# Hybrid decoder step on one core: embedding products around the routing's rank and table, and two pieces of VectorE work moved

## What is computed

```
x = x + token_mix(rmsnorm(x))               # convolution and retention heads
h = rmsnorm(x)
gate, eid = top-1 of 4 groups, then top-2 of its 8 experts, per token
x = x + sum over the 2 picks of gate * (silu(h Wg[e]) * (h Wu[e])) Wd[e]    # 32 experts
ple = rmsnorm(p @ w_ple)                    # the embedding product
x = x + ple * sigmoid(x @ w_ple_gate);  y = rmsnorm(x)
```

## Time and profile before

| | us |
|---|---|
| median of 3 runs | 692.29 (692.18 to 695.29) |
| profiled execution | 691.82 |
| its span, first to last instruction | 690.0 |
| TensorE, VectorE, ScalarE, GpSimd busy | 661.9, 575.8, 405.4, 259.7 |
| mean granted TensorE clock | 0.987 of full |

### The profile page before, as it was taken

One profiled execution on the slowest core, in us unless ns is written; L12 is line 12 of the kernel. 1 busy time (PEld: TensorE's weight loads), 2 busy tenths in 40 slices (PEclk: granted clock), 3 DMA queues, 4 the chain that ended last, 5 costly groups with the idle time before them and its releaser, 6 DMA issues.

```text
span 690.0 us, 12915 instructions
## 1 busy us (share of the span) xinstructions
PE 661.9 (96%) x4714; PEld 605.8 (88%) x4714; DVE 575.8 (83%) x808; ACT 405.4 (59%) x521; POOL 259.7 (38%) x182
## 2 busy tenths in 40 slices
PE   7999999998999999997999999999999999998995
PEld 5899999998998979956899999999999999876885
DVE  5499999996866484476889999999999999969785
ACT  7331242227263042366789999999999999853322
POOL 1131588979428330005233333333333333320001
PEclk9999999999999999989999999999999999999998
DMA  9641432112019263536699999999999999676211
GB/s 292 200 139 19 150 111 74 62 63 73 1 65 343 85 217 120 207 144 210 258 341 376 371 364 371 361 369 379 384 392 387 381 388 382 251 312 207 77 61 62
DMA packets 49534, 156.14 MB, mean 226 GB/s; under 512 B 6938, under 2 KB 28634, under 8 KB 36427
## 3 DMA queue, kind: packets, MB, share of 16 engines
q1 hardware_dynamic: 35905, 133.98, 52.3%
q10 hardware_dynamic: 9346, 12.13, 5.2%
q0 software_dynamic: 4240, 9.44, 4.0%
HBM read 143.55 MB, written 17.59 MB: 234 GB/s over the span
## 4 chain that ended last, share of the span: by engine, by line
PE 73%; DVE 9%; issue 5%; POOL 4%; DMA 4%; ACT 2%; ACTq 0%; SPq 0%; POOLq 0%; DVEq 0%
PE bank L606 70%; PE bank L610 4%; DMA out<-front 1%; DMA catT<-expert_rows 1%; DVE front L1756 1%; POOL uext L2289 1%; DVE front L1757 1%; DVE z L1392 1%; DVE front L1783 1%; DVE z L1564 1%; POOL z L2376 1%; DVE z L1700 1%; DMA scratch<-h_rows,sorted_tok 1%; POOL grs L2369 1%; POOL uext L2288 1%
## 5 line engine op out<-in xcount | busy, mean ns | idle before, releaser
L1425 DVE TENSOR_TENSOR ring_parts<-ring,catT_parts 128x2048 fp32r<-128x2048 f32 x64 | 146.2, 2285 | 0.6 <-ACT catT_parts L2016 0.5
L2016 ACT ACTIVATE catT_parts<-ring 128x2048 fp32r<-128x2048 f32 x64 | 123.3, 1926 | 5.7 <-PE bank L606 5.7
L606 PE MATMUL bank<-ring_parts,hT_high 128*128 128x256 f32 (+1 forms) x748 | 113.7, 296 | 0.0
L2422 POOL DMA_INDIRECT expert_rows<-scratch,cur_code x32 | 40.8, 1274 | 172.3 <-issue 121.5
L606 PEld LDWEIGHTS bank<-ring_parts,hT_high 128*128 128x128 f32 x748 | 100.6, 189 | 4.0 <-DVE ring_parts L1295 0.2
L1264 DVE SCALAR_TENSOR_TENSOR bank<-uext,cpar,bank 128x512 f32<-128x512 f32 x116 | 87.4, 753 | 0.0
L1614 DVE TENSOR_TENSOR ring_parts<-ring,down_high 128x2048 fp32r<-128x2048 f32 x30 | 68.8, 2293 | 8.1 <-ACT down_high L2118 7.4
L2269 POOL TENSOR_TENSOR ring_parts<-ring,ring_parts 128x2048 fp32r<-128x2048 f32 x11 | 51.7, 4701 | 60.0 <-ACT ring_parts L1831 60.0
L606 PE MATMUL bank<-ring_parts,catT_parts 128*128 128x256 f32 x480 | 69.2, 282 | 2.5 <-DVE front_parts L1321 1.3
L606 PE MATMUL bank<-catT_parts,xT_odd 128*128 128x256 f32 x512 | 67.8, 285 | 0.0
L2398 POOL COPY cur_code<-codes 128x1 int32 (+1 forms) x32 | 63.2, 1976 | 7.9 <-DVE tokidx L1551 7.7
(11 more groups left out here) (342 smaller groups left out, 1318.5 us busy)
## 6 DMA issues: line engine op xcount, KB each, us to landing
ring<-in_w_expert_gate SPq DMA_DIRECT2D x32, 1024.0 KB, 5.5
ring<-in_w_expert_up SPq DMA_DIRECT2D x32, 1024.0 KB, 5.8
ring<-in_w_expert_down SPq DMA_DIRECT2D x32, 1024.0 KB, 5.3
ring<-in_w_in SPq DMA_DIRECT2D x12, 1024.0 KB, 7.1
ring<-in_w_out SPq DMA_DIRECT2D x4, 1024.0 KB, 4.8
ring<-in_w_ple_gate SPq DMA_DIRECT2D x4, 1024.0 KB, 9.8
catT<-in_x_prompt SPq DMA_DIRECT2D x4, 512.0 KB, 4.9
z<-in_x_prompt SPq DMA_DIRECT2D x4, 512.0 KB, 5.3
```

What stands on the lines that cost most here:

```text
L606: return nc.tensor.matmul(out, lhsT, rhs, start=start, stop=stop, skip_group_check=True)
L1425: V.tensor_tensor(ring_r[:, 3 * par + m, :], ring[:, 3 * par + m, :], cat_r[:, m * CHUNK:(m + 1) * CHUNK].bitcast(F32), ALU.subtract).then ...
L2016: A.activation(cat_r[:, m * CHUNK:(m + 1) * CHUNK], ring[:, s, :], ACT.Copy).then_inc(S["w_hi"], 1)
L2422: G.indirect_dma_start(moe_d, bass.IndirectOffsetOnAxis(ap=cur_code[0:r, par:par + 1], axis=0), yout[0:r, par, :], None, bounds_check=2 * ...
```

## The change

On TensorE, `ple_tile(1)` and `ple_tile(3)` are made in halves: the rank stands between the halves of tile 1 instead of behind it, the sort table between the halves of tile 3 instead of behind it. The 14 `idle_products` ahead of the first gathered block are gone. The slot table is multiplied behind the last transposes of gathered blocks instead of between the gate products and block 1. On VectorE, `w_low(0, 0, 0)` moves from ahead of the routing to behind the decode of the sort table, and `slots` is cut in two: `slot_places` stays, now behind `w_low(0, 0, 0)`; `slot_one_hots` is made later, behind `w_low(0, 0, 1)` and ahead of the copies of blocks 1 to 3. `sorted_T(1)`, which takes over bank 7, waits for the last reader of the rank there (`picks_done` 3) instead of the one-hots.

```diff
@@ TensorE @@
-            ple_tile(1)
+            ple_tile(1, (0,))
...
             m.then_inc(S["rank_done"], 1)
+            ple_tile(1, (1,))
             ple_tile(2)
-            ple_tile(3)
+            ple_tile(3, (0,))
...
             table(laneone, sortone, NT, 2)
+            ple_tile(3, (1,))
             ple_tile(4)
...
                 if t == 1:
-                    pe.wait_ge(S["one_hot"], 3)
+                    pe.wait_ge(S["picks_done"], 3)
...
-            idle_products(14, 4)
             pe.wait_ge(S["ple_raw"], 2 * TT)
             pe.wait_ge(S["idx_done"], 1)
             sorted_T(0)
             gate_up(0, 0, (0,))
-            table(slotone, blockone, NBLK, 4)
             for t in range(1, 4):
                 sorted_T(t)
             gate_up(0, 0, (1,))
             for t in range(4, NT):
                 sorted_T(t)
+            table(slotone, blockone, NBLK, 4)
             hid_T(0, 0)
@@ VectorE @@
             V.memset(even32, -EVEN).then_inc(S["zeroed"], 1)
-            w_low(0, 0, 0)
             dve.wait_ge(S["logit_done"], TT)
...
-            def slots():
+            def slot_places():
 
                 then(V.tensor_scalar(ov, rp[:, TT, :], 1.0, -(SLOTS + 1) / 2, ALU.max, ALU.add))
-                V.tensor_tensor(prod2, M, bc(rp[:, 0:TT, :], 1, 2), ALU.mult)
+                V.tensor_tensor(prod2, M, bc(rp[:, 0:TT, :], 1, 2), ALU.mult).then_inc(S["picks_done"], 1)
...
                 then(V.tensor_tensor(posb, posb, pick_w, ALU.add))
+
+            def slot_one_hots():
+
                 then(V.tensor_tensor(blockeq, bc(C("block"), 1, 2 * TT), bc(posb.rearrange("p k i -> p (k i)"), 2, NBLK),
                                      ALU.is_equal))
...
-            slots()
+            w_low(0, 0, 0)
+            slot_places()
...
+            slot_one_hots()
             for t in range(1, 4):
                 sorted_half(t)
             w_low(0, 1, 0)
```

## The result

| | kernel before | changed kernel |
|---|---|---|
| median of 20 runs each | 692.56 us (690.21 to 695.29) | 694.27 us (691.18 to 696.41) |
| ratio, 95% interval | | 1.0026 (1.0014 to 1.0039) |
| profiled span | 690.0 us | 691.7 us |
| mean granted clock in the profile | 0.987 | 0.983 |

The change costs 0.26%, or 1.8 us (1.0 to 2.7): within 0.5%, as forecast, and in the direction forecast. A second set of 12 runs beside 35 of the kernel before gave 1.0020 (1.0002 to 1.0039).

The account below looks back on a forecast made before the run. TensorE, busy throughout each expert step, was taken as the bound, so only the loop's start shifts: + 0.35 (one-hots) + 0.65 (slot table) = + 1.0 us. Between 692.8 (profiled) and 693.3 (median), forecast 693.2 us, range 691.0 to 695.4.

Parts of the forecast that it names:

- three signs: Wrong if ScalarE waits for the first transposes, block 1's copy waits for TensorE, or up products show clock 0.5.
- rival (a): Rows land 1.20 us early, ScalarE isn't in the way, one-hots fit idle VectorE time: - 0.55, 691.7 us; chance 0.15.
- rival (b): ScalarE's lateness is taken up before block 1; slot table saves 0.65 there, costs 0.65 later: zero, 692.3 us; chance 0.17.
- Rank, split tiles, decode: TensorE: rank waits for ScalarE's pT copies, scan 1.20 us earlier; sort decode at 311.12 instead of 312.32.
- ScalarE late: ScalarE's embedding copies and table load move by 1.16 us; with 0.75 of slack, block 0's copy is 0.41 late.
- First gather: GpSimd: moved subtraction may delay the issue; rows land between 316.98 and 318.18, late end taken, at no cost.
- The first transposes and the gate products: TensorE: gate products start at 321.03 instead of 320.62 and take the same 4.48 us, ending at 325.51.
- rival (c): Without idle products TensorE runs at 1.2 GHz through the up products: + 4.7, 697.0 us; gates alone 0.9; chance 0.13.
- The hold: VectorE's slot one-hots, 2.59 us, delay the copy of block 1 by 0.35; transposes of block 3 wait for it.
- The slot table's 0.65: TensorE: slot table stands between the last transposes and step (0, 1) with nothing to hide it: + 0.65 us.

Follow-up runs that it names:

- experiment 1: Changed kernel with the 14 idle products put back ahead of the first gathered block; ratio 1.0008 (0.9980 to 1.0036) to the kernel before.
- experiment 2: Changed kernel with the first low gate part back in its old place ahead of the routing; ratio 1.0009 (0.9984 to 1.0035).
- experiment 3: Changed kernel with slot one-hots back behind the places and slot table back between gate products and block 1; ratio 1.0002 (0.9977 to 1.0027).
- experiment 5: Kernel before with its 14 idle products taken out and nothing else; ratio 1.0008 (0.9980 to 1.0037).
- experiment 9: Changed kernel with 14 idle products back and ScalarE's table load moved forward behind tile 1's copies; ratio 1.0011 (0.9994 to 1.0029).
- experiment 6: Changed kernel with 30 idle products ahead of the first transposes and 12 behind them; ratio 1.0051 (1.0032 to 1.0070).
- 12: Changed kernel again, with no edit, 12 runs beside 35 of the kernel before; ratio 1.0020 (1.0002 to 1.0039).
- 4: Changed kernel with tiles 1 and 3 whole again, rank behind tile 1, sort table behind tile 3; ratio 1.0033 (1.0004 to 1.0061).
- experiment 10: Kernel before with 30 and 12 idle products, weight loads held until the last gather has landed; ratio 1.0014 (1.0000 to 1.0029).
- experiment 11: Changed kernel, 30 and 12 idle products, subtraction and one-hots back, table load earlier, slot table between blocks 7 and 8, weight loads held; ratio 0.9996 (0.9973 to 1.0020).

## Why the prediction was right, and which term was too small

**The number and the path.** Forecast for the time was + 0.9 us, measured + 1.8 (1.0 to 2.7, so less than 0.5% could be told from no change after all), and the stretch grew by more than forecast in both profiles. Two of the three signs by which I would be wrong did show: ScalarE's copy of block 0 waited for TensorE (0.54 and 0.34 us), and in the first profile the copy of block 1 did too (0.62). Neither came the way of rival (a) or (b), which had nothing lost: TensorE was late there because its clock was low. So the queues were counted rightly, but the wait that ended last at block 0, and in the first profile at block 1, was not the one that I named, and that the sum fits as well as it does is partly luck.

**Rank, split tiles, decode.** Right to 0.1 us: the rank 3.56 us into the stretch (3.47 predicted) with ScalarE's pT copies as releaser, the decode at 11.51 (11.41).

**ScalarE late.** Right: its table load 1.31 later than before (1.16 predicted). Where ScalarE was the one to set block 0's copy (experiments 1 to 3), the gates came 0.56 late for its sake (0.41 predicted), and moving the load took 0.46 of that back.

**First gather.** The late end that I took was right within 0.3 us: the subtraction holds the issue (2.39 us with it, 1.31 without). That it costs nothing held only where the transposes ran at the full clock (experiments 1 and 3). The Trainium skill, SBUF — State Buffer, section Who interferes with whom, infers that such a subtraction leaves descriptor writing alone, while it does hold up what GpSimd reads from SBUF. A gather's issue also reads its row numbers there; the runs show the hold, not which of the two it is.

**The first transposes and the gate products: the term that was too small.** I had the copy of block 0 start no earlier than ScalarE is free, with the transposes done by then at 1.13 us, and the gates at the same 4.48 as before. TensorE had gone without products for over 3 us before the transposes, and in both profiles they ran at 1.2 GHz, in 1.94 us: with the rows 0.3 later or less, block 0 was copied 1.10 and 0.87 late, not 0.41. The gates took 5.29 in one profile, wholly at 1.2 GHz, and 4.39 in the other. That is rival (c) in part: its 0.9 for the gates came true at times, its low clock in the up products never did. The Trainium skill, TensorE: Matmul & The Clock Gate, Part 1, with the throttled state as the default, agrees with the low transposes. The idle products' removal brought them: experiment 5 shows it alone (1.13 to 1.94). In all eight profiles with idle products ahead the transposes took 1.05 to 1.14 us; in the six without, 1.94 in four, 1.60 in experiment 2 and 1.13 in experiment 3. For the gates 14 idle products do not settle it: 4.48 us before, 5.24 in experiment 1, 3.49 at the full clock in experiment 9. That full clock gives 3.5 us and not the 2.78 of my lower bound: in experiment 6 TensorE was busy for 3.23 and waited for VectorE's low part for most of the rest.

**One-hots, slot table.** The hold was right where the gates' clock came back (0.31 to 1.51 us of waiting for VectorE in experiments 2, 6, 9 and 12) and absent where they ran low to the end or nearly so (the first profile, experiments 1 and 4). Low clock and hold are thus alternatives, not a sum: in experiment 6 the gates were 1.74 us faster than in experiment 1 and step (0, 1) came at 38.66 in place of 38.84. The slot table's 0.65 ahead of step (0, 1) is there (1.86 us from block 8 to step (0, 1), against 1.13), but where nothing holds block 3 it comes back behind the gates, as rival (b) had it.

**The clock in the times.** Over the 35 executions of the kernel before beside experiments 1 to 4, the time falls by 0.47 us for each 0.001 of mean granted clock (correlation -0.82). The changed kernel's mean was 0.9838 over its 20 runs, the kernel before's 0.9862 and 0.9869 in the two larger sets: 0.0024 to 0.0031 less, or 1.1 to 1.5 us of the 1.8. That is a correlation between executions of one kernel, and between kernels it fails: experiment 3 had 0.0020 less clock than the kernel before beside it and 0.15 us more between the means, experiment 6 0.0019 more clock and 2.7 us more. That the low clock costs time at this place is shown in the traces only.

**What stays open.** The intervals of experiments 1 to 3 overlap with both kernels, so how the 1.8 us split between clock and queues isn't shown by times. And the stretch, shorter by 1.0 in experiment 10 and 1.9 in 11, brought no time, so that 1.8 us of time stands beside 1.4 and 2.3 of stretch proves little. Behind the loop the two profiles were 2.6 and 3.5 us longer than that of before (experiment 11: 92.4 against 88.9 us from the last gate products to the end). The last rows scattered by the loop, from issue to landing, before and in experiment 11:

```profile
616.46 2.62 DMA expert_rows<-scratch,cur_code
```

```profile
615.57 3.68 DMA expert_rows<-scratch,cur_code
```

In the five kernels with 30 and 12 idle products this took 3.56 to 3.93 us, in the nine others 2.48 to 2.69, and the first transposes behind the loop came 24.4 to 24.9 us after the last gate products instead of 23.3 to 23.5. So about 1 us is lost there in each of the five; why is open. The rest goes with the clock behind it: in the 20 us that begin 20 us after the last gate products it was 1.00 in the profiles of the kernel before and of experiment 2, 0.91 in four and 0.83 in the other eight, among them experiments 1, 3, 4 and 5. What decides that clock is not shown.

## What to carry to other kernels

A piece moved off one engine's path is late on the next: count each engine's queue up to the point where they meet, and take the latest, not the sum. Products that compute nothing may be holding the clock for what follows them; see what runs behind them before taking them out. A shorter path may start loads earlier, into transfers that were alone before. And follow a shorter stretch to the end of the kernel before calling it a gain.

## What was not expected of the hardware

Twelve idle products more between the first transposes and the gates, with sixteen more ahead, made the kernel before 4.8 us slower between the means; a gather of rows that met weight loads of 1 MB took up to 10.6 us to land (7.2 at most before), and holding the loads until the gathers were in took nearly all of it back (ratio 1.0092 to 1.0014). And a GpSimd gather's issue took 2.39 us beside a VectorE subtraction with two inputs in SBUF, against 1.31 without.
